# Row numbers of the gathered experts from one sum over two key numbers, the first kept scaled by 128, in a two-layer decoder kernel on one core

## Chip, core and metric

The kernel runs on one core of one Trainium2 chip. The metric is device time of one execution in microseconds (us), lower is better. The engines are named as in the profile: PE (TensorE, matrix products; PEld its weight loads), DVE (VectorE), ACT (ScalarE), POOL (GpSimd) and SP, which only starts transfers.

## What is computed

Two layers: RWKV time mixing, then a pooling mixer, each followed by an expert layer ("PEER") with 8 heads. The change is in the expert layers alone. A head scores two sets of 128 keys, keeps the best 16 of each, adds them pairwise and keeps the best 16 of the 256 sums. Each kept pair names one of 16384 experts, and the expert's number is first key times 128 plus second key:

```
s_top, i_top = lax.top_k(s, K)
cand = (s_top[..., 0, :, None] + s_top[..., 1, None, :]).reshape(B, S, PEER_HEADS, K * K)
cand_idx = (i_top[..., 0, :, None] * N_KEYS + i_top[..., 1, None, :]).reshape(B, S, PEER_HEADS, K * K)
best, pos = lax.top_k(cand, K)
idx = jnp.take_along_axis(cand_idx, pos, axis=-1)
gate = jax.nn.softmax(best, axis=-1).astype(h.dtype)
...
u_sel = jnp.take(u_tab, ix, axis=0)
act = jax.nn.gelu(jnp.einsum('thkd,td->thk', u_sel, hx), approximate=False)
v_sel = jnp.take(v_tab, ix, axis=0)
return jnp.einsum('thk,thkd->td', gx * act, v_sel)
```

## The kernel before

`phase_peer` runs once per layer (tiles named `peer0...`, `peer1...`). Tokens lie on 128 partitions in four tiles. For the first two and a half token tiles nothing is gathered: all 128 tiles of the table U are multiplied with the tokens on PE (`u_product`, L2076, 24 products of 320 columns for each tile e), and the gates are spread into a dense matrix later. For the last tile (GT) and half of the one before (OT) the rows of U are gathered: POOL starts an indirect transfer for each of the head's numbers (`fetch_u`, L2297, 512 KB into one of 8 buffers `row`) and DVE multiplies each row with its token (`dot`, L2381).

In the first 56 tiles the eight heads run beside this, one for each HEAD_TILES = 7 tiles. For head n:

- PE makes the query (L2053 to L2055), one u_product, then the scores (L2062), then six more u_products. ACT takes the scores into `sc` (L2180); windows below are cut at these moments.
- For each tile ACT rounds U into `uhi` (L2168) and POOL makes the remainder `ulo` (L2320, in `low_u`), which u_product waits for. POOL's order is fixed: a remainder, then one to three `fetch_u`; twice in a head also the remainder of the next query's weights `wlo` (L2326, right behind an `ulo`).
- DVE looks for the best 16 of both sides (L2412 to L2416), adds the pairs (L2428), turns the key numbers `pos` into bfloat16 `posf` (L2431), looks for the best 16 pairs, and finds each pair's two ranks (L2436 to L2445). Then for s = 0, 1: a 0/1 mask of ranks (L2448), times the key numbers or their steps `posd` (L2450), summed over 16 (L2451) into `slots[:, 1 + s]`. L2452 makes first number x 128 + second, L2454 adds the layer's offset and stores integers in `idx`, which signals `idx_made`. Twelve dots of a previous head are laid between these steps by `fill`.

DVE's order is written out: the next head starts with a search (L2412) and then one dot. `fetch_u(m)` waits for the head's numbers and for the dot eight before it, since there are NG = 8 buffers. So POOL, in front of a fetch, can wait for a dot of DVE, and PE waits behind POOL for the remainder.

After the heads `slots` is turned by PE, and ACT takes it into `slotT` (`take_slots`, L2194), where `slotT[:, 1]` must be the plain first key number: DVE compares it with 0 to 127 (L2480).

Of the kernel before, what the change touches and what calls it, by code (L numbers as in the profile page):

```python
# [15 lines left out]
ALU = mybir.AluOpType  # L16
ACT = mybir.ActivationFunctionType
AX = mybir.AxisListType

P = 128  # L20
HEAD = 64
TOPK = 16
# [1736 lines left out]
def phase_peer(nc, made, const, arena, kept, pe_t, name, layer, w_q, keysT, uT, u_rows, v_tab, v_rows, mod_rows, w_dram, gelu_dram,  # L1759
# [4 lines left out]
    with ExitStack() as ctx:  # L1764
# [4 lines left out]
        DT, GT = TT - 1, TT - 1  # L1769
        SD = DT * P  # L1770
        HEADS = w_q.shape[0]
        SLOTS = HEADS * TOPK
        ET = uT.shape[0]
# [69 lines left out]
        slotT = arena("slotT", [P, 3, SD])  # L1843
# [33 lines left out]
        posf, posd = early("posf", [P, 2, TT, TOPK + 2], BF16), early("posd", [P, TT, TOPK], BF16)  # L1877
        starts = early("starts", [P, 2, TOPK])
        best, bpos = early("best", [P, TT, TOPK]), early("bpos", [P, TT, TOPK], U32)
        half_u, half_f = early("half_u", [P, 2, TT * TOPK], U32), early("half_f", [P, 2, TT * TOPK])  # L1880
        total = early("total", [P, TT * HEADS])
        slots = early("slots", [P, 3, TT, SLOTS])
        idx_f = early("idx_f", [P, 2, TOPK])
        h_rows = [kept["gate"], kept["g_row"]]
# [54 lines left out]
        with nc.Block() as block:  # L1939
# [216 lines left out]
            def _(act):  # L2156
# [35 lines left out]
                def take_slots(q):  # L2192
                    act.wait_ge(slots_turned, q + 1)
                    a.activation(slotT[:, q], four[q % 2][:, 0:SD], ACT.Copy).then_inc(slotT_made, 1)  # L2194

# [165 lines left out]
            def _(dve):  # L2361
# [7 lines left out]
                ch.send(v.tensor_tensor(h_own, x_own, h_rows[0][:], ALU.add))  # L2369
                ch.send(v.memset(posf[:, :, :, 0:2], 0.0))  # L2370
                ch.send(v.tensor_scalar(starts[:, 1], const["iota"][:, 0:TOPK], float(FULL_ROWS * (FULL_ROWS - 1)), None, ALU.add))
                ch.wait()
# [45 lines left out]
                for n in range(HEADS):  # L2418
# [7 lines left out]
                    for rows_of, cols_of, to in ((slice(0, FULL_ROWS), TOPK, slice(0, at)), (slice(FULL_ROWS, TOPK), FULL_ROWS, slice(at, CAND))):  # L2426
# [3 lines left out]
                                                val[:, 1, :, 0:cols_of].unsqueeze(2).to_broadcast(shape), ALU.add))  # L2430
                    v.tensor_copy(posf[:, :, :, 2:], pos[:]).then_inc(less_made, 1)  # L2431
                    ch.wait()
# [13 lines left out]
                    for s, (ranks, op, by) in enumerate(((starts[:, 0], ALU.is_le, posd[:]), (const["iota"][:, 0:TOPK], ALU.is_equal, posf[:, 1, :, 2:]))):  # L2446
# [4 lines left out]
                        ch(v.tensor_reduce(slots[:, 1 + s, :, col], hot[:, s], AX.X, ALU.add))  # L2451
                    ch(v.scalar_tensor_tensor(out=idx_f[:], in0=slots[:, 1, OT:GT + 1, col], scalar=float(P), in1=slots[:, 2, OT:GT + 1, col],  # L2452
                                              op0=ALU.mult, op1=ALU.add))
                    v.tensor_scalar(idx[:, :, col], idx_f[:], float(layer * ET * P), None, ALU.add).then_inc(idx_made, 1)  # L2454
                v.sem_inc(all_less, 1)
# [216 lines left out]
```

## Time and profile before

| | us |
|---|---|
| median of 3 runs | 3241.31 (3236.23 to 3244.79) |
| the profiled execution | 3236.63 |
| its span, first to last instruction | 3234.8 |
| PE busy | 3041.8 |
| DVE busy | 2671.3 |
| POOL busy | 2173.7 |
| ACT busy | 1413.9 |
| heads and what follows up to the softmax, layer 0 | 601 to 942 |
| the same, layer 1 | 1987 to 2328 |

A row of the profile gives a busy time; for DVE and POOL that includes time in which a started instruction doesn't get on. So the same instruction's shortest and longest durations are worth comparing. A wait that hangs on several signals is put down to the one that came last by the profile, which need not be the one that mattered.

### The profile page before, as it was taken

What the parts mean: (1) busy time and instruction counts of PE and PEld (TensorE: products, weight loads), DVE (VectorE), ACT (ScalarE), POOL (GpSimd) and SP (SyncE); (2) the same over time, 40 slices, a digit from 0 to 9 for tenths busy, and PEclk for the clock granted to TensorE, in tenths of its full rate; (3) what the DMA queues carried; (4) which work ended last, traced back from release to release, by engine and by line L of the source; (5) the groups of instructions that cost most, each with busy time, mean ns of one, the idle gap of its engine ahead of it and who ended that gap; (6) DMA issues with size and microseconds to landing.
All of it is one profiled execution on the core that took longest, in us unless ns stands there. A gap on an engine that the chain in (4) does not pass through costs nothing. (4 is left out here: it accounts for less than half of the span.)

```text
span 3234.8 us, 58229 instructions
## 1 busy us (share of the span) xinstructions
PE 3041.8 (94%) x21401; PEld 2588.8 (80%) x21401; DVE 2671.3 (83%) x4637; ACT 1413.9 (44%) x2848; POOL 2173.7 (67%) x1430
## 2 busy tenths in 40 slices
PE   8999998999988889999999899999898899999998
PEld 3347887788888889888888677888888898888886
DVE  8775663699998775999999656899988768999997
ACT  0124553433347776333333423333377763333333
POOL 1223543588887777888888505888877678888884
PEclk9999999999999999999999999999999999999999
DMA  9950011588888999999999505888889999999994
GB/s 343 323 192 16 4 52 51 194 315 294 276 297 320 368 372 339 362 339 338 356 337 338 202 29 163 305 298 279 285 309 368 387 336 362 337 337 353 339 337 172
DMA packets 370430, 891.65 MB, mean 276 GB/s; under 512 B 39769, under 2 KB 191889, under 8 KB 363026
## 3 DMA queue, kind: packets, MB, share of 16 engines
q1 hardware_dynamic: 266514, 511.04, 45.4%
q0 software_dynamic: 103680, 377.53, 32.2%
q8 instruction: 139, 2.28, 0.3%
q14 instruction: 97, 0.79, 0.1%
HBM read 801.19 MB, written 86.03 MB: 274 GB/s over the span
## 5 line engine op out<-in xcount | busy, mean ns | idle before, releaser
L2076 PE MATMUL peer_acc<-peer_hhi,peer_uhi 128*128 128x320 f32 x2048 | 657.1, 321 | 42.0 <-POOL peer0same_ulo L2320 22.1
L2076 PE MATMUL peer_acc<-peer_hlo,peer_uhi 128*128 128x320 f32 x2048 | 642.4, 314 | 0.0
L2381 DVE SCALAR_TENSOR_TENSOR peer_row<-peer_row,peer_acc 128x1024 f32<-128x1024 f32 x384 | 462.8, 1209 | 91.1 <-DMA peer_row<-in_pe_u,peer_idx 84.7
L2076 PEld LDWEIGHTS peer_acc<-peer_hhi,peer_uhi 128*128 128x128 f32 x2048 | 394.4, 193 | 51.1 <-POOL peer0same_ulo L2320 26.1
L2076 PEld LDWEIGHTS peer_acc<-peer_hlo,peer_uhi 128*128 128x128 f32 x2048 | 394.1, 192 | 1.0 <-issue 0.5
L2320 POOL TENSOR_TENSOR peer1same_ulo<-ahead_u,peer_uhi 128x1024 fp32r<-128x1024 f32 x128 | 314.8, 2462 | 100.9 <-ACT peer_uhi L2168 97.3
L2320 POOL TENSOR_TENSOR peer0same_ulo<-ahead_u,peer_uhi 128x1024 fp32r<-128x1024 f32 x128 | 313.8, 2455 | 99.1 <-ACT peer_uhi L2168 93.4
L2349 POOL TENSOR_TENSOR peer1lsame_vlo<-peer1l_v,peer_uhi 128x1024 fp32r<-128x1024 f32 x128 | 308.6, 2411 | 76.3 <-ACT peer_uhi L2217 75.7
L2349 POOL TENSOR_TENSOR peer0lsame_vlo<-peer0l_v,peer_uhi 128x1024 fp32r<-128x1024 f32 x128 | 308.4, 2409 | 75.2 <-ACT peer_uhi L2217 74.1
L2392 DVE SCALAR_TENSOR_TENSOR peer_acc<-peer_row,peer_p_g,peer_acc 128x1024 f32<-128x1024 f32 x254 | 324.5, 1278 | 18.4 <-DMA peer_row<-in_pe_v,peer_idx 18.0
L2076 PE MATMUL peer_acc<-peer_hhi,peer1same_ulo 128*128 128x320 f32 x1024 | 321.5, 314 | 0.0
L2076 PE MATMUL peer_acc<-peer_hhi,peer0same_ulo 128*128 128x320 f32 x1024 | 320.0, 312 | 0.0
L2119 PE MATMUL peer_acc<-peer_uhi,peer1p_phi 128*128 128x512 f32 x768 | 299.4, 390 | 4.3 <-DVE peer1lo_plo L2508 2.8
L2119 PE MATMUL peer_acc<-peer_uhi,peer0p_phi 128*128 128x512 f32 x768 | 299.2, 390 | 3.7 <-DVE peer0lo_plo L2508 2.3
L2119 PE MATMUL peer_acc<-peer_uhi,peer1lo_plo 128*128 128x512 f32 x768 | 298.8, 389 | 0.0
L2119 PE MATMUL peer_acc<-peer1lsame_vlo,peer1p_phi 128*128 128x512 f32 x768 | 298.8, 389 | 0.0
L2119 PE MATMUL peer_acc<-peer0lsame_vlo,peer0p_phi 128*128 128x512 f32 x768 | 298.8, 389 | 0.0
L2119 PE MATMUL peer_acc<-peer_uhi,peer0lo_plo 128*128 128x512 f32 x768 | 298.8, 389 | 0.0
L2297 POOL DMA_INDIRECT peer_row<-in_pe_u,peer_idx x256 | 257.1, 1004 | 59.7 <-issue 51.2
L2297 POOL DMA_INDIRECT peer_row<-in_pe_v,peer_idx x256 | 261.2, 1020 | 38.9 <-issue 9.3
L2164 ACT ACTIVATE peer_gel<-peer_acc 128x320 f32<-128x320 f32 x256 | 110.1, 430 | 398.8 <-PE peer_acc L2076 385.5
L2168 ACT ACTIVATE peer_uhi<-ahead_u 128x1024 fp32r<-128x1024 f32 x250 | 262.1, 1048 | 0.0
(522 smaller groups left out, 7241.5 us busy)
## 6 DMA issues: line engine op xcount, KB each, us to landing
ahead_u<-in_pe_uT SPq DMA_DIRECT2D x256, 512.0 KB
peer0l_v<-in_pe_v SPq DMA_DIRECT2D x128, 512.0 KB
peer1l_v<-in_pe_v SPq DMA_DIRECT2D x128, 512.0 KB
activations<-peer_gel SPq DMA_DIRECT2D x256, 160.0 KB
rw_g<-in_ada POOLq DMA_DIRECT2D x60, 512.0 KB
routing<-peer0m_wb SPq DMA_DIRECT2D x20, 1024.0 KB
peer0l_wt<-routing SPq DMA_DIRECT2D x64, 320.0 KB
routing<-peer1m_wb SPq DMA_DIRECT2D x20, 1024.0 KB
```

The lines of the kernel that those rows point to most:

```text
L2076: mm = pe.matmul(ub[e % 2][:, 0:UD], a, h[:, k, 0:UD], start=(n == 0), stop=(n == 3 * KT - 1))
L2119: mm = pe.matmul(acc[:, t, ds], a[:, ts], w[:, ds], start=(begin and n == 0), stop=(end and n == 2), skip_group_check=True)
L2164: a.activation(gel[:, e % NL], ub[e % 2][:, 0:UD], ACT.Gelu).then_inc(gel_made, 1)
L2168: a.activation(uhi[:, n % NH], u[:, n % NU], ACT.Copy).then_inc(uhi_made, 1)
L2297: g.indirect_dma_start(row[:, at % NG], None, table, bass.IndirectOffsetOnAxis(ap=of, axis=0)).then_inc(row_loaded[at % NG], 16)
L2320: g.tensor_tensor(ulo[:, q].rearrange("p k e -> p (k e)"), u[:, q].rearrange("p k e -> p (k e)"), uhi[:, e % NH].bitcast(F32).rearrange("p ...
L2349: g.tensor_tensor(vlo[:, q], vr[:, q], vhi[e % NH].bitcast(F32), ALU.subtract).then_inc(vlo_made, 1)
L2381: v.scalar_tensor_tensor(out=row[:, m % NG], in0=row[:, m % NG], scalar=1.0, in1=h_own if mine else h_g, op0=ALU.mult, op1=ALU.mult, accum ...
L2392: v.scalar_tensor_tensor(out=acc_g, in0=row[:, at % NG], scalar=p_g[:, s:s + 1], in1=acc_g, op0=ALU.mult, op1=ALU.add).then_inc(acc_made, 1)
```

## The change

The first key number is scaled when it becomes a float: `posf[:, 0]` is now key x 128 plus layer x 16384, in an instruction of its own (`tensor_scalar`), and `posf[:, 1]` in another (`tensor_copy`); before, one instruction made both. All these values are whole numbers of at most 8 significant bits times a power of two, so bfloat16 holds them. The steps `posd`, the mask products and the sums work as before on the scaled numbers. The expert's number is then one `tensor_reduce` over the two sums, stored as integers, in place of two instructions with a wait between. `slotT[:, 1]` is scaled back by ACT, with Identity, a scale of 1/128 and a bias from `first_key`, a [128, 1] tile set once in each layer.

```diff
-        starts = early("starts", [P, 2, TOPK])
+        starts, first_key = early("starts", [P, 2, TOPK]), early("first_key", [P, 1])
...
                     act.wait_ge(slots_turned, q + 1)
-                    a.activation(slotT[:, q], four[q % 2][:, 0:SD], ACT.Copy).then_inc(slotT_made, 1)
+                    if q == 1:
+                        a.activation(slotT[:, q], four[q % 2][:, 0:SD], ACT.Identity, scale=1.0 / P, bias=first_key[:]).then_inc(slotT_made, 1)
+                    else:
+                        a.activation(slotT[:, q], four[q % 2][:, 0:SD], ACT.Copy).then_inc(slotT_made, 1)
...
                 ch.send(v.memset(posf[:, :, :, 0:2], 0.0))
+                ch.send(v.memset(first_key[:], float(-layer * ET)))
...
-                    v.tensor_copy(posf[:, :, :, 2:], pos[:]).then_inc(less_made, 1)
+                    v.tensor_copy(posf[:, 1, :, 2:], pos[:, 1])
+                    v.tensor_scalar(posf[:, 0, :, 2:], pos[:, 0], float(P), float(layer * ET * P), ALU.mult, ALU.add).then_inc(less_made, 1)
...
-                    ch(v.scalar_tensor_tensor(out=idx_f[:], in0=slots[:, 1, OT:GT + 1, col], scalar=float(P), in1=slots[:, 2, OT:GT + 1, col],
-                                              op0=ALU.mult, op1=ALU.add))
-                    v.tensor_scalar(idx[:, :, col], idx_f[:], float(layer * ET * P), None, ALU.add).then_inc(idx_made, 1)
+                    with nc.allow_low_precision(reason="whole numbers below 2 ** 24, exact in float32, kept as integers"):
+                        v.tensor_reduce(idx[:, :, col], slots[:, 1:3, OT:GT + 1, col].rearrange("p s t k -> p t k s"), AX.X,
+                                        ALU.add).then_inc(idx_made, 1)
```

DVE, layer 1, end of a head and start of the next, before (`hot` is the mask, `slots` the sums, `peer_row` a gathered row):

```order
L2450 TENSOR_TENSOR peer1a_hot<-peer1a_hot,peer1a_posf 128x1024
L2451 TENSOR_REDUCE peer1a_slots<-peer1a_hot 128x4x16
L2452 SCALAR_TENSOR_TENSOR peer1a_idx_f<-peer1a_slots 128x32
L2454 TENSOR_SCALAR peer_idx<-peer1a_idx_f 128x2x16
L2412 MAX peer1a_val<-peer1a_sc 128x8 x4
L2381 SCALAR_TENSOR_TENSOR peer_row,peer_dots<-peer_row,peer_acc 128x1024
```

The same place after (line numbers are 3 to 4 higher):

```order
L2454 TENSOR_TENSOR peer1a_hot<-peer1a_hot,peer1a_posf 128x1024
L2455 TENSOR_REDUCE peer1a_slots<-peer1a_hot 128x4x16
L2457 TENSOR_REDUCE peer_idx<-peer1a_slots 128x2x16
L2415 MAX peer1a_val<-peer1a_sc 128x8 x4
L2384 SCALAR_TENSOR_TENSOR peer_row,peer_dots<-peer_row,peer_acc 128x1024
```

Two instructions of DVE have become one, of another kind; the search and the first dot follow it as before.

DVE in the middle of a head of layer 1, after, where one CAST of 128x8x16 (L2431) stood between the pair sums and the search:

```order
L2431 TENSOR_TENSOR kept_b_row<-peer1a_val 128x4x64
L2431 TENSOR_TENSOR kept_b_row<-peer1a_val 128x4x48
L2434 CAST peer1a_posf<-peer1a_pos 128x4x16
L2435 TENSOR_SCALAR peer1a_posf<-peer1a_pos 128x4x16
L2415 MAX peer1a_best<-kept_b_row 128x8 x4
```

One instruction more. ACT, layer 0, behind the heads (`peer0a_slots` is the softmax's exponential), after:

```order
L2264 ACTIVATE peer0a_slots<-peer0a_slots 128x512
L2163 ACT_TABLE_LOAD
L2163 ACTIVATE peer_gel<-peer_acc 128x320
L2167 ACTIVATE peer_uhi<-ahead_u 128x1024
L2196 ACTIVATE peer_slotT<-peer_acc 128x384
L2194 ACTIVATE peer_slotT<-peer_acc,peer0a_first_key 128x384
```

The table load stood there before too; none is added. The orders of PE, POOL and SP are unchanged, and `first_key`'s memset in each layer is the only other new instruction.

## Rows read from the trace of the kernel before

**Rows 1.** The page, the chain that ended last, by line.
```profile
PE peer_acc L2119 15%; DVE peer_row L2381 3%; PE peer_acc L2076 3%; POOL peer_row L2297 2%; DMA peer_row<-in_pe_u,peer_idx 1%; POOL peer1same_ulo L2320 1%; DVE peer1a_idx_f L2452 1%; DVE peer1a_hot L2448 1%; PE peer_acc L2051 0%; DVE peer1a_slots L2451 0%; DVE peer1a_pos L2416 0%; DVE peer1a_pos L2414 0%; DVE kept_g_row L2413 0%; DMA kept_g_row<-activations 0%; DVE kept_b_row L2428 0%
```

**Rows 2.** Busy time of each engine in windows from scores taken to scores taken.
```profile
core 0: us, PE busy (x) PEld busy (x) DVE busy (x) ACT busy (x) POOL busy (x), PEclk, DMA share, GB/s
681.50:719.68 38.18, 37.59 (x235) 35.43 (x234) 37.87 (x136) 13.79 (x22) 33.82 (x21) 1.00 0.91 310
719.68:886.99 167.31, 155.53 (x931) 146.19 (x930) 165.70 (x551) 55.12 (x82) 136.75 (x84) 0.97 0.85 288
2066.58:2104.74 38.16, 37.58 (x235) 35.42 (x234) 37.82 (x137) 13.79 (x22) 33.39 (x21) 1.00 0.92 311
2104.74:2272.94 168.20, 158.03 (x931) 149.12 (x930) 166.58 (x552) 55.13 (x82) 136.50 (x84) 0.95 0.85 286
2272.94:2328.24 55.30, 49.26 (x328) 47.66 (x327) 53.75 (x145) 19.09 (x29) 47.57 (x27) 1.00 0.86 304
```

**Rows 3.** Timeline of DVE (start, us, ...) from one head's start to the next's.
```profile
2115.59 0.87 DVE L2412 MAX8 peer1a_val<-peer1a_sc 128x8 f32<-128x128 f32 x4
...
2148.41 2.06 DVE L2448 TENSOR_TENSOR peer1a_hot<-const_made,peer1a_half_f 128x1024 bf16<-128x1024 f32 x1
...
2152.48 4.91 DVE L2452 SCALAR_TENSOR_TENSOR peer1a_idx_f<-peer1a_slots 128x32 f32<-128x32 f32 x1
...
2157.52 0.86 DVE L2412 MAX8 peer1a_val<-peer1a_sc 128x8 f32<-128x128 f32 x4
2158.30 1.20 DVE L2381 SCALAR_TENSOR_TENSOR peer_row<-peer_row,peer_acc 128x1024 f32<-128x1024 f32 x1
```

**Rows 4.** Timeline of POOL over the same place, and one of the tail.
```profile
2152.56 2.42 POOL L2320 TENSOR_TENSOR peer1same_ulo<-ahead_u,peer_uhi 128x1024 fp32r<-128x1024 f32 x1
2154.94 2.40 POOL L2326 TENSOR_TENSOR peer1aover_wlo<-ahead_wq,peer1aover_whi 128x1024 fp32r<-128x1024 f32 x1
2160.29 0.95 POOL L2297 DMA_INDIRECT peer_row<-in_pe_u,peer_idx_own  x1 [2.95 <-DMA peer_idx_own<-peer_idx]
...
2284.47 0.95 POOL L2297 DMA_INDIRECT peer_row<-in_pe_u,peer_idx_own  x1 [2.96 <-DVE peer_row L2381]
```

**Rows 5.** Timeline of PE: the gap behind POOL in two heads.
```profile
2085.22 0.41 PE L2076 MATMUL peer_acc<-peer_hhi,peer_uhi 128*128 128x320 f32 x1 [0.58 <-POOL peer1same_ulo L2320]
...
2163.67 0.41 PE L2076 MATMUL peer_acc<-peer_hhi,peer_uhi 128*128 128x320 f32 x1 [2.71 <-POOL peer1same_ulo L2320]
```

**Rows 6.** DVE's groups by line: xcount | busy us, mean ns | idle before.
```profile
L2452 DVE SCALAR_TENSOR_TENSOR peer0a_idx_f<-peer0a_slots 128x32 f32<-128x32 f32 x8 | 25.0, 3127 | 0.3
L2452 DVE SCALAR_TENSOR_TENSOR peer1a_idx_f<-peer1a_slots 128x32 f32<-128x32 f32 x8 | 23.6, 2945 | 0.3
```

**Rows 7.** Line L2451: duration ns min/median/max, first and last start, forms.
```profile
L2451 DVE TENSOR_REDUCE peer1a_slots<-peer1a_hot x16: 1219/1220/1222, 2014.8 to 2322.7; 128x64 f32<-128x1024 bf16 x16
```

**Rows 8.** Timelines of DVE and POOL in the head in front, layer 1.
```profile
2071.16 0.19 DVE L2452 SCALAR_TENSOR_TENSOR peer1a_idx_f<-peer1a_slots 128x32 f32<-128x32 f32 x1
...
2089.96 2.90 DVE L2428 TENSOR_TENSOR kept_b_row<-peer1a_val 128x256 f32<-128x256 f32 x2
...
2101.83 0.22 DVE L2436 TENSOR_TENSOR peer1a_slots<-peer1a_best 128x64 f32<-128x64 f32 x1
...
2089.89 2.40 POOL L2320 TENSOR_TENSOR peer1same_ulo<-ahead_u,peer_uhi 128x1024 fp32r<-128x1024 f32 x1
```

**Rows 9.** Timeline of DVE: other instructions held up, first and last head.
```profile
2002.08 2.44 DVE L2431 CAST peer1a_posf<-peer1a_pos 128x128 bf16<-128x128 uint32 x1
...
2319.86 2.78 DVE L2450 TENSOR_TENSOR peer1a_hot<-peer1a_hot,peer1a_posf 128x1024 bf16<-128x1024 bf16 x1
```

**Rows 10.** Timelines of DVE and ACT behind the last head.
```profile
2330.20 0.69 DVE L2460 TENSOR_REDUCE peer1a_total<-peer1a_slots 128x32 f32<-128x512 f32 x1 [2.87 <-ACT peer1a_slots L2262]
...
2328.24 1.28 ACT L2262 ACT_TABLE_LOAD   x1
```

More of the change, by code:

```diff
@@ L1882, in phase_peer @@
         slots = early("slots", [P, 3, TT, SLOTS])
-        idx_f = early("idx_f", [P, 2, TOPK])
         h_rows = [kept["gate"], kept["g_row"]]
```

## Prediction

> **What bounds the kernel now.** I read the page's chain first. A line that only turns 512 sums into 256 numbers, L2452, holds 1% of the span in it, as much as a line with far more work [rows 1]. Its group says why: 16 instructions take 25.0 + 23.6 = 48.6 us, 3.0 us each for 32 numbers [rows 6], while the undisturbed one takes 0.19 us [rows 8]. So about 48.6 - 16 x 0.19 = 45.6 us of DVE's time are spent standing, spread over both layers.
>
> The timelines say what it stands for. In the head that begins at 2115.59, L2452 starts at 2152.48 and lasts 4.91 us, to 2157.39 [rows 3]. POOL runs two subtractions without a break from 2152.56 to 2157.34 [rows 4]. DVE goes on when POOL's second one ends. L2451, the sum over one tensor just ahead of it, takes 1.219 to 1.222 us in all of its cases, in every head and whatever POOL does [rows 7]; L2452, L2450, L2448 and L2431 are the ones with long cases [rows 3, 9]. What is held up is an instruction that reads two tensors, or a copy; a sum over one tensor isn't.
>
> Next, who waits for DVE. The windows from scores to scores tell it: four heads take 168.20 us in layer 1, with DVE busy 166.58 of them, PE 158.03, POOL 136.50 [rows 2]. DVE is the engine without idle time. The way to PE leads through POOL: the next head's first dot (L2381) starts at 2158.30 and ends 1.2 us later, and POOL starts the fetch that needs its buffer at 2160.29, 2.95 us late. The profile puts that down to the move of the numbers, but the same wait in another head is put down to the dot (2.96), and 2158.30 + 1.20 + 0.79 = 2160.29 [rows 3, 4]; I take the dot. POOL's remainder then comes late and PE stands 2.71 us [rows 5]. In these four heads PE's granted clock is 0.95 on average, some of the time at its 1.2 GHz level, against 1.00, all at 2.4 GHz, in the head in front [rows 2]. I don't count that apart, since it lies inside the windows' difference.
>
> **A head without the stall** is in the trace: in the head whose L2452 took 0.19 us [rows 8] the next scores came after 38.16 us, in layer 0 after 38.18 [rows 2]; PE's gap was 0.58 us [rows 5]. The following four take 168.20 / 4 = 42.05 and 167.31 / 4 = 41.83 us. These two quiet windows are my yardstick.
>
> **Part by part.**
> Removed, L2452: 0.19 us of own time and the standing in it, 4.72 us in the head of rows 3.
> Removed, L2454: own time 0.18, of which 2157.52 - 2157.39 = 0.13 us lies on the path [rows 3].
> Added, the sum into `idx`: 64 elements read. The nearest rows are a sum over 512 numbers, 0.69 us [rows 10], and one over 1024, 1.22 us [rows 7]; a line through both gives 0.16 us fixed and 1.04 ns a number, so 0.22 us. Its bounds are 0.1 us and 0.69 us, the upper one because its two inputs lie far apart in memory, which no row shows. I take 0.22: even 0.69 would cost 8 x 0.5 us a layer of slack that isn't used up (below). By rows 7 it doesn't stand behind POOL; if it does, that is the second rival.
> Added, a second instruction for `posf`: 0.1 us between two starts, as L2454 to the next. Below nothing it can't be, since work is added; above, an instruction of this place (L2431) has taken 2.44 us [rows 9], 2.2 more than when free. I take 0.13 and keep 2.2 for a rival.
> Added on ACT: Identity with a scale and a bias for one copy of PSUM per layer. No table load is added in the order; if one were, it would be 1.28 us [rows 10], so 0 to 2.6 us in all. I take 0. The memset per layer is far ahead of any wait: 0.
>
> DVE's own time per head, from search to search: 2157.52 - 2115.59 = 41.93 [rows 3]. Of it 4.72 is L2452's stall, and L2448 took 2.06 where the free mask takes 1.22, so 0.84. That leaves 36.37, and the edits make 36.37 - 0.19 - 0.13 + 0.22 + 0.13 = 36.4 us. So DVE alone could do a head in 36.4, and PE and POOL do one in 38.2. DVE can stand 1.8 us per head elsewhere before it sets the time again.
>
> Will it stand more? I follow the phases. Count from the moment at which scores are taken. The quiet head ends for DVE at about 2110.6 + 0.3, 6.1 us behind the scores of 2104.74 (the stall of 4.7 us then made it 10.85: 2115.59). L2428 stood at 18.5 us after its head's start, 2089.96, against a subtraction of POOL that ran 23.3 to 25.7 us behind the scores (2089.89, 2.40 long) [rows 8]. With a lag of 6.1 DVE comes there at 24.6 and stands 1.1 us. The closing row of small instructions (L2436) starts 9.65 us of work later, at 6.1 + 28.15 + 1.1 - 38.2 = 2.85 us ahead of the next scores; in the quiet head that was 2104.74 - 2101.83 = 2.91, and what followed there was the 0.84 us at L2448, in the head of rows 3 too. Sum 1.9 us, so the next lag is 6.1 + 36.4 + 1.9 - 38.2 = 6.2. A larger lag misses POOL's subtraction at L2428 and shrinks; a smaller one meets more of it and grows. The phase holds itself, and DVE is then just not the bound. POOL's first fetch that needs a dot comes 2157.5 - 2146.4 = 11.1 us behind the scores, and the dot is done and seen 2.8 us after the head's start, so any lag below 8.3 us leaves POOL free.
>
> **What is late next** is PE with POOL: 38.2 us, plus 0.2 that I allow for DVE's longer `posf` and for phases that are not just those of the quiet head. The sum:
> layer 0, four heads: 167.31 - 4 x 38.4 = 13.7 us;
> layer 1, four heads: 168.20 - 4 x 38.4 = 14.6 us;
> the stretch of 55.30 us behind the last scores in each layer [rows 2]: POOL's wait of 2.96 in it goes [rows 4], and POOL sets the pace of the tiles there, so up to 3.0 us; I take 2 in each, 4 us.
> Together 32 us. The first three heads keep their times. What stands behind the heads starts earlier and has no other change. Against its own execution that is 3236.6 - 32.3 = 3204.3 us. That execution lies 4.7 us below the median of the runs (3241.3), so for a median I say **3209 us**.
>
> **The rivals.**
> First, the phase doesn't hold and half of the gain is eaten: L2428, L2448 and L2450 stand 3 to 4 us a head in place of 1.9, DVE needs 36.4 + 3.5 = 39.9. For it: in the heads at both ends of each layer such stalls are common (2.22 at L2428 in rows 8; 2.09 at L2450 and 2.2 at L2431 in rows 9). The eight heads take 167.31 + 168.20 = 335.5 now, so 335.5 - 8 x 39.9 = 16 us: 3225.
> Second, no change: the stall moves. POOL's double subtraction is still there, and the instruction ahead of L2452, the product L2450, can meet it, or the new sum stands as L2452 did. At 5.5 us a head DVE needs 41.9 as now, and 3241 stays. For it: 0.84 + 4.72 = 5.56 is just what it stands now, so a mere move gives nothing. Against it: the sum over one tensor never stood [rows 7], and from a lag of 6 the product is done some 2 us before the double subtraction begins.
> A rule of the Trainium skill leads to the same end by another way. "VectorE: DVE Perf Modes", section "Rules for kernel authors", says that chained operations of this engine are not to be fused for speed, and that the number of operations is what to cut; it adds that a reduce is the slowest kind. Per head the change takes away three (a copy, L2452, L2454) and puts in three. By that count it would be worth nothing. The rows speak against the count as a measure here: what goes is not an operation's own 0.2 us.
> Third, slower. The extra instruction for `posf` and a lag that grows meet: if a head in front loses so much that DVE starts over 8.3 us behind the scores, POOL is held again, and if L2450 comes to stand for both subtractions, there are still 1.22 + 0.22 us of sums behind it, where now only L2452's last 0.2 us follow. The head would need about 42 + 1.2, ten heads 12 us more, plus 2.2 us where `posf` is caught: 3255. The point is a lag of 8.3 in place of 6.1, so 2.2 us more of stalls in one head than the quiet one had (2.22 at L2428 and 0.84 at L2448). Beside this stands a rule of the skill, "SBUF — State Buffer", section "SBUF: two separate sides": VectorE and GpSimd share a port pair that one of them holds for a whole instruction, and copies that use both read ports need it as well. That is why a second copy is a second chance to be caught; it gives no price that the rows lack.
> Fourth, more than the forecast: PE's gap and POOL's holds go entirely, heads take PE's own 37.6 [rows 2]: 335.5 - 300.8 = 34.7 and 6 in the tails, 41 us: 3200.
>
> **How the numbers follow.** My forecast (3204 to 3219; the ends are 38.0 us a head with 6 us in the tails, and 39.2 with none) has 0.5, the first rival 0.18, no change 0.15, slower 0.09, more than the forecast 0.08. A change within 0.3%, 10 us, is about what a measurement of this kernel can't tell from none. Faster by more: 0.5 + 0.08 + 0.18 = 0.76; within: 0.15; slower: 0.09. The range leaves out the slower case and the half of no change that lies above: 3199 to 3238.
>
> **What would show it.** The new sum (L2457) in 0.2 us in all 16 heads. Windows between scores of 38 to 38.6 us from the fourth head on, PE's clock back at 1.00 where its gap falls from 2.7 to about 0.6. POOL's 2.95 us in front of a fetch gone. DVE with gaps or with under 2 us of stalls per head at L2431, L2452 and L2454 of the new file. I am wrong if L2457 has cases of 2 us and more (second rival), if the products and masks show the 4.7 us instead (second or third), or if the heads shorten and the tiles behind them lengthen.

## The result: slower by 27 us, and the profile after

The kernel before takes 3239.46 us (median of 4 runs, 3236.23 to 3244.79), the changed one 3266.7 us (median of 4, 3264.8 to 3272.68). The ratio is 1.0085, with a 95% interval of 1.0072 to 1.0098: slower by 0.85%, some 27 us, where the prediction said 3209 and gave "slower" a chance of 0.09. The profiled execution of the changed kernel took 3264.8 us with a span of 3263.0 us.

The lines of the change come first. The two sources L2452 and L2454 of before are gone. In their place stands L2457, and the one copy for `posf` is now L2434 (copy, second keys) and L2435 (scaled, first keys). From the views of single lines (durations in ns as min/median/max, then the first and last start):

```profile
L2457 DVE TENSOR_REDUCE peer_idx<-peer0a_slots x8: 222/224/229, 633.7 to 951.8; 128x32 uint32<-128x64 f32 x8
L2457 DVE TENSOR_REDUCE peer_idx<-peer1a_slots x8: 222/224/228, 2038.1 to 2353.3; 128x32 uint32<-128x64 f32 x8
...
L2435 DVE TENSOR_SCALAR peer0a_posf<-peer0a_pos x8: 180/3020/3032, 620.5 to 929.0; 128x64 bf16<-128x64 uint32 x8
L2435 DVE TENSOR_SCALAR peer1a_posf<-peer1a_pos x8: 181/3022/3032, 2022.9 to 2331.1; 128x64 bf16<-128x64 uint32 x8
```

The sum is as cheap as was estimated, 0.22 us in all 16 heads. The scaled half of `posf` has 64 elements per partition and takes 0.18 us when nothing is in its way, but its median is 3.02 us. That is a stall of 2.84 us, in the same five of the eight heads of each layer (the third to the seventh), with next to no spread between them.

The windows from scores to scores say where the time goes. The columns are as in [rows 2]: window, us, busy time of each engine, PE's granted clock, DMA share, GB/s.

```profile
680.42:718.58 38.16, 37.59 (x235) 35.43 (x234) 38.06 (x129) 13.79 (x21) 33.34 (x21) 1.00 0.90 313
718.58:897.30 178.72, 158.04 (x931) 149.40 (x930) 177.21 (x553) 55.13 (x81) 137.25 (x84) 0.92 0.80 269
897.30:957.90 60.60, 53.10 (x328) 51.77 (x327) 53.96 (x154) 19.10 (x29) 46.24 (x27) 0.92 0.81 278
2082.78:2120.92 38.14, 37.58 (x235) 35.42 (x234) 38.04 (x129) 13.79 (x21) 33.37 (x21) 1.00 0.91 312
2120.92:2299.72 178.80, 158.91 (x931) 150.27 (x930) 177.29 (x555) 55.14 (x81) 137.21 (x84) 0.92 0.81 270
2299.72:2357.60 57.88, 50.63 (x328) 49.02 (x327) 53.05 (x152) 19.09 (x29) 46.95 (x27) 0.97 0.84 289
```

Against [rows 2], the head in front of the four is unchanged (38.16 and 38.14 against 38.18 and 38.16). The four heads take 178.72 and 178.80 where they took 167.31 and 168.20, so 11.4 and 10.6 us more. The stretch behind the last scores takes 60.60 and 57.88 instead of 55.30, so 5.3 and 2.6 more. Together that is 29.9 us; the spans differ by 3263.0 - 3234.8 = 28.2. A head now lasts 178.8 / 4 = 44.7 us, with DVE busy 177.3 of 178.8, so DVE is still the engine without idle time. PE's clock is 0.92 on average in these heads (0.97 and 0.95 before), more of the time at its 1.2 GHz level, after longer gaps.

What stands in one of these heads is in DVE's timeline (start, us, engine, line). First the place where `posf` is made, then the closing block:

```profile
2197.93 0.70 DVE L2431 TENSOR_TENSOR kept_b_row<-peer1a_val 128x256 f32<-128x256 f32 x2
...
2198.54 0.20 DVE L2434 CAST peer1a_posf<-peer1a_pos 128x64 bf16<-128x64 uint32 x1
2198.64 3.03 DVE L2435 TENSOR_SCALAR peer1a_posf<-peer1a_pos 128x64 bf16<-128x64 uint32 x1
...
2211.18 2.28 DVE L2447 TENSOR_SCALAR peer1a_half_u<-peer1a_half_u 128x64 uint32<-128x64 uint32 x1
...
2217.25 2.53 DVE L2452 TENSOR_TENSOR peer1a_hot<-const_made,peer1a_half_f 128x1024 bf16<-128x1024 f32 x1
2219.82 2.78 DVE L2454 TENSOR_TENSOR peer1a_hot<-peer1a_hot,peer1a_posf 128x1024 bf16<-128x1024 bf16 x1
2222.62 1.22 DVE L2455 TENSOR_REDUCE peer1a_slots<-peer1a_hot 128x64 f32<-128x1024 bf16 x1
2223.88 0.22 DVE L2457 TENSOR_REDUCE peer_idx<-peer1a_slots 128x32 uint32<-128x64 f32 x1
```

and POOL beside it:

```profile
2197.99 1.20 POOL L2299 DMA_INDIRECT peer_row<-in_pe_u,peer_idx_own  x1 [0.16 <-issue]
2199.21 2.40 POOL L2322 TENSOR_TENSOR peer1same_ulo<-ahead_u,peer_uhi 128x1024 fp32r<-128x1024 f32 x1
...
2216.30 2.41 POOL L2322 TENSOR_TENSOR peer1same_ulo<-ahead_u,peer_uhi 128x1024 fp32r<-128x1024 f32 x1 [0.24 <-ACT peer_uhi L2167]
2218.66 3.38 POOL L2328 TENSOR_TENSOR peer1aover_wlo<-ahead_wq,peer1aover_whi 128x1024 fp32r<-128x1024 f32 x1
2226.78 0.95 POOL L2299 DMA_INDIRECT peer_row<-in_pe_u,peer_idx_own  x1 [4.74 <-DMA peer_idx_own<-peer_idx]
```

L2435 starts at 2198.64, inside the fetch that began at 2197.99, and ends at 2201.67, with the subtraction that ended at 2201.61. So it stood through the rest of the fetch and the whole subtraction. In the closing block of the same head three instructions stand, with their free durations beside them: L2447 2.28 (0.19 for its like), L2452 2.53 (1.22), L2454 2.78 (0.69). The stalls are 2.1, 1.3 and 2.1, so 5.5 us in place of the 5.56 of before (4.72 at old L2452 and 0.84 at L2448, [rows 3]). The standing at the key numbers has gone, and nearly the same amount has come back in front of the sums. The extra 2.84 comes on top. With 36.4 us of own work that makes 36.4 + 2.8 + 5.5 = 44.7, the mean of the four measured heads (this one takes 44.56 from search to search, 2179.46 to 2224.02). POOL now waits 4.74 us at the fetch that needs the first dot (2.95 before, [rows 4]), and PE's gap behind it is 4.82 us (2.71 before, [rows 5]):

```profile
2230.17 0.63 PE L2075 MATMUL peer_acc<-peer_hhi,peer_uhi 128*128 128x320 f32 x1 [4.82 <-POOL peer1same_ulo L2322]
```

### The profile page after: what moved, and what is told of

Same layout as the page of the kernel before. It is cut to its first block and busy times, and to the rows that moved or that the text cites. A ratio compares the mean times of both kernels' runs of the same rounds, so it can differ in the third digit from the quotient of the medians.

```text
span 3263.0 us, 58231 instructions
## 1 busy us (share of the span) xinstructions
PE 3046.2 (93%) x21401; PEld 2593.0 (79%) x21401; DVE 2700.4 (83%) x4639; ACT 1413.6 (43%) x2848; POOL 2168.5 (66%) x1430
## 3 DMA queue, kind: packets, MB, share of 16 engines
q8 instruction: 139, 2.28, 0.3%
## 5 line engine op out<-in xcount | busy, mean ns | idle before, releaser
L2075 PE MATMUL peer_acc<-peer_hhi,peer_uhi 128*128 128x320 f32 x2048 | 660.3, 322 | 63.1 <-POOL peer0same_ulo L2322 32.1
L2075 PE MATMUL peer_acc<-peer_hlo,peer_uhi 128*128 128x320 f32 x2048 | 645.5, 315 | 0.0
L2075 PEld LDWEIGHTS peer_acc<-peer_hhi,peer_uhi 128*128 128x128 f32 x2048 | 397.6, 194 | 70.8 <-POOL peer0same_ulo L2322 35.4
L2075 PEld LDWEIGHTS peer_acc<-peer_hlo,peer_uhi 128*128 128x128 f32 x2048 | 397.5, 194 | 1.0 <-issue 0.5
L2075 PE MATMUL peer_acc<-peer_hhi,peer0same_ulo 128*128 128x320 f32 x1024 | 322.5, 315 | 0.0
L2075 PE MATMUL peer_acc<-peer_hhi,peer1same_ulo 128*128 128x320 f32 x1024 | 322.1, 315 | 0.0
L2299 POOL DMA_INDIRECT peer_row<-in_pe_u,peer_idx x256 | 250.2, 978 | 59.6 <-issue 51.0
```

Of the source, the lines that this page charges most:

```text
L2075: mm = pe.matmul(ub[e % 2][:, 0:UD], a, h[:, k, 0:UD], start=(n == 0), stop=(n == 3 * KT - 1))
L2299: g.indirect_dma_start(row[:, at % NG], None, table, bass.IndirectOffsetOnAxis(ap=of, axis=0)).then_inc(row_loaded[at % NG], 16)
```

## The experiments

My theory after the result had two parts. The one sum is worth what was predicted. The second `posf` instruction costs more than that, because it stands for POOL's fetch and the subtraction behind it. The rivals were that the sum is the cause, that the number of instructions is, or that any extra instruction in this place has this price. Eight kernels were run. The kernel before ran beside them and gave medians of 3241.22, 3242.56 and 3238.41 us. All kernels compute the whole result.

| kernel | key numbers | `posf` | us | ratio to before (95%) |
|---|---|---|---|---|
| changed kernel | one sum | copy, then scaled | 3266.7 | 1.0085 (1.0072 to 1.0098) |
| split_only | as before | copy, then times 1 | 3271.19 | 1.0097 (1.0081 to 1.0114) |
| one_posf | one sum | one product | 3210.28 | 0.9906 (0.9889 to 0.9922) |
| late_scale | one sum | one copy, differences scaled later | 3216.19 | 0.9924 (0.9907 to 0.9941) |
| swap_posf | one sum | scaled, then copy | 3266.12 | a single run |
| posf_first | one sum | copy and scaled, ahead of the pair sums | 3209.1 | 0.989 (0.9873 to 0.9906) |
| split_reduce | as before | copy, then a sum over an axis of one | 3244.76 | 1.0006 (0.9996 to 1.0015) |
| one_first | one sum | one product, ahead of the pair sums | 3209.5 | 0.9897 (0.9881 to 0.9914) |
| late_split | one sum | copy, then a sum over an axis of one | 3211.66 | 0.9917 (0.99 to 0.9933) |

### split_only: the split without the sum

From the kernel before:

```diff
-                    v.tensor_copy(posf[:, :, :, 2:], pos[:]).then_inc(less_made, 1)
+                    v.tensor_copy(posf[:, 1, :, 2:], pos[:, 1])
+                    v.tensor_scalar(posf[:, 0, :, 2:], pos[:, 0], 1.0, 0.0, ALU.mult, ALU.add).then_inc(less_made, 1)
```

> The kernel before with one edit: posf is made by two instructions (a copy and a tensor_scalar times 1), the numbers still by L2452 and L2454. Theory A (the second instruction is what costs: POOL's fetch and the subtraction behind it get in between the two): the tensor_scalar lasts about 3.0 us in the middle heads, heads of 43.5 us or more, some 10 x 2 to 10 x 2.9 us slower than before, 3258 to 3268. Theory B (the loss comes from taking L2452 away, whose wait kept DVE and POOL in a good phase): within 5 us of 3239.

It measured 3271.19 us, so 30 us slower than before with this one edit, and 3 us over the range expected. The split alone carries the whole loss, and it costs slightly more than the changed kernel. DVE's groups (busy us, mean ns | idle before) show something unexpected too:

```profile
L2432 DVE TENSOR_SCALAR peer1a_posf<-peer1a_pos 128x64 bf16<-128x64 uint32 x8 | 17.9, 2239 | 0.0
...
L2453 DVE SCALAR_TENSOR_TENSOR peer1a_idx_f<-peer1a_slots 128x32 f32<-128x32 f32 x8 | 2.4, 298 | 0.3
```

L2453 is the instruction that held 4.7 us per head before (mean 2945 ns, [rows 6]). Here it is still in the program, and it takes 298 ns. Its long wait left it without being taken out: after its stand at `posf`, DVE comes to the closing block 2.8 us later than before in relation to POOL, so POOL's subtractions met the mask and the product ahead of it (L2449 at 2.71, L2451 at 2.78 us in the head of 2174.82) and a small instruction (L2445, 2.41 us). This is why the changed kernel gets nothing from removing it: where a second instruction stands at `posf`, L2452 has no wait left to remove.

### one_posf: the sum without the split

From the changed kernel, with a tile `key_by` of two columns that holds 128 and 1, and the layer's offset in a column of `posf` that is read for the first difference:

```diff
+                ch.send(v.memset(posf[:, 0, :, 1:2], float(-layer * ET * P)))
...
-                    v.tensor_copy(posf[:, 1, :, 2:], pos[:, 1])
-                    v.tensor_scalar(posf[:, 0, :, 2:], pos[:, 0], float(P), float(layer * ET * P), ALU.mult, ALU.add).then_inc(less_made, 1)
+                    v.tensor_tensor(posf[:, :, :, 2:], pos[:], key_by[:].unsqueeze(2).unsqueeze(3).to_broadcast([P, 2, TT, TOPK]),
+                                    ALU.mult).then_inc(less_made, 1)
```

> The changed kernel with one edit: posf is made by one instruction again, a tensor_tensor of pos with a [128, 2] tile that holds 128 and 1; the layer's offset comes in through the zero column in front of the steps. The numbers still come from one sum. Theory A: heads of 38.2 to 38.6 us from the fourth on, 3205 to 3215 in all, as I had predicted for the whole change. Theory B: the wait moves into the closing block (5.4 us a head there, as in the changed kernel), heads of 41.5 us or more, 3235 to 3267.

It measured 3210.28 us, 31 us faster than before, with the same result as the changed kernel. This is close to the 3209 that the prediction gave to the change. All four heads and one of them:

```profile
2129.10:2167.99 38.89, 37.85 (x235) 35.43 (x234) 38.51 (x138) 13.79 (x22) 34.25 (x21) 1.00 0.91 316
2090.17:2245.74 155.57, 151.41 (x931) 141.71 (x930) 154.06 (x549) 55.16 (x82) 136.90 (x84) 1.00 0.89 310
```

A head takes 38.9 us with PE at full clock; the prediction had 38.4, and 38.6 was the most expected before the run. The two layers' four heads take 155.57 and 155.00 us, the stretches behind them 52.92 and 52.93. Against [rows 2] that is 12.6 + 12.3 + 2.4 + 2.4 = 29.7 us less; the spans differ by 28.4.

With split_only this fills a table of four, each against the kernel before that ran beside it: the sum without the split -31; the split alone +30; both +27. If the effects added, both together would give -1. They don't add: what the sum saves is saved only while DVE's lag behind the scores stays small, and a second instruction that stands makes it large.

### late_scale: one copy, the scale put elsewhere

From the changed kernel:

```diff
+                ch.wait()
+                ch.send(v.memset(posf[:, 0, :, 1:2], float(-layer * ET)))
...
-                    v.tensor_copy(posf[:, 1, :, 2:], pos[:, 1])
-                    v.tensor_scalar(posf[:, 0, :, 2:], pos[:, 0], float(P), float(layer * ET * P), ALU.mult, ALU.add).then_inc(less_made, 1)
+                    v.tensor_copy(posf[:, :, :, 2:], pos[:]).then_inc(less_made, 1)
...
                     ch(v.tensor_tensor(posd[:], posf[:, 0, :, 2:], posf[:, 0, :, 1:TOPK + 1], ALU.subtract))
+                    ch.send(v.tensor_scalar(posd[:], posd[:], float(P), None, ALU.mult))
```

> The changed kernel with the scaling at another place: one copy makes posf unscaled, as before the change, and a tensor_scalar of 64 numbers multiplies the steps posd by 128 in the closing block, where several short instructions follow each other. As many instructions as in the changed kernel. Theory A: the place counts, not the number; no 3 us at posf, heads near 38.5 to 39, 3205 to 3220. Theory B: 3235 to 3267. A third theory, that one more instruction anywhere costs: about as the changed kernel, 3260 to 3270.

It measured 3216.19 us, with heads of 38.9 us. This kernel has as many DVE instructions per head as the changed one, and the scaling is an instruction of its own as there. At its new place it stands in one head of eight in each layer (2.28 us; the mean is 444 ns, the median 182). So neither the number of instructions nor the scaling costs the 27 us; the place does.

### swap_posf: the same two, the other way round

```diff
+                    v.tensor_scalar(posf[:, 0, :, 2:], pos[:, 0], float(P), float(layer * ET * P), ALU.mult, ALU.add)
+                    v.tensor_copy(posf[:, 1, :, 2:], pos[:, 1]).then_inc(less_made, 1)
```

> The changed kernel with the two instructions for posf in the other order, the tensor_scalar first. Theory A says the second one, now the copy, lasts 3.0 us in the middle heads and the time stays 3265. If it is the kind of instruction that is held up, the tensor_scalar has the long cases in first place too, and the copy none.

It measured 3266.12 us in a single run, as the changed kernel. The long cases changed their owner:

```profile
L2435 DVE CAST peer0a_posf<-peer0a_pos 128x64 bf16<-128x64 uint32 x8 | 17.9, 2242 | 0.0
...
L2434 DVE TENSOR_SCALAR peer0a_posf<-peer0a_pos 128x64 bf16<-128x64 uint32 x8 | 3.8, 470 | 0.0
```

In the third to the seventh head of each layer, whichever of the two comes second lasts 3.02 us and the first 0.2. As between a copy and a scaling, it is the second place and not the kind.

### posf_first: the same two, some 0.7 us earlier

The two `posf` lines of the changed kernel are moved ahead of the pair sums, and nothing else.

> The changed kernel with its two instructions for posf put ahead of the two pair sums (L2431) instead of behind them; nothing else. Theory A1 (it is the order of asking: POOL's fetch starts with DVE's row of four instructions, needs the port about half a microsecond later, and gets it at the first gap between two instructions that it has asked before): at that time DVE is in its last long pair sum, after which DVE asks for nothing, so there is no 2.85 us at posf; heads of 38.5 to 39, 3208 to 3220. Theory A2 (a fourth instruction in the row is one too many, wherever it stands): the last of the four stands 2.8 us and the time stays 3260 to 3270.

It measured 3209.1 us, 58 us below the changed kernel, with the same instructions (the profiled execution was the slowest of its four, 3219.74 us). From the second head of each layer on, the copy now stands for the subtraction that is already running (in place of the pair sums behind it), and the scaled one takes 0.18 us. DVE and POOL in one head (layer 1; start, us):

```profile
2161.66 2.41 POOL L2322 TENSOR_TENSOR peer1same_ulo<-ahead_u,peer_uhi 128x1024 fp32r<-128x1024 f32 x1
2162.38 1.75 DVE L2428 CAST peer1a_posf<-peer1a_pos 128x64 bf16<-128x64 uint32 x1
2164.05 0.18 DVE L2429 TENSOR_SCALAR peer1a_posf<-peer1a_pos 128x64 bf16<-128x64 uint32 x1
2164.15 0.68 DVE L2433 TENSOR_TENSOR kept_b_row<-peer1a_val 128x256 f32<-128x256 f32 x2
2164.23 1.16 POOL L2299 DMA_INDIRECT peer_row<-in_pe_u,peer_idx_own  x1 [0.16 <-issue]
```

When the fetch starts, both `posf` instructions are done. Behind the pair sums comes a search, which POOL doesn't hold up (the searches over `kept_b_row`, one by one, take 250 to 268 ns in all 64 cases of the changed kernel). This is the cleanest run against the rival that counts instructions. A rule of the Trainium skill leads to that rival: "VectorE: DVE Perf Modes", section "Rules for kernel authors", says to minimise the count of operations. By that rule the changed kernel and posf_first would take the same time; they differ by 58 us at the same count.

### split_reduce: the split, with a second instruction of another kind

From the kernel before:

```diff
-                    v.tensor_copy(posf[:, :, :, 2:], pos[:]).then_inc(less_made, 1)
+                    v.tensor_copy(posf[:, 1, :, 2:], pos[:, 1])
...
+                        v.tensor_reduce(posf[:, 0, :, 2:], pos[:, 0].unsqueeze(3), AX.X, ALU.add).then_inc(less_made, 1)
```

> The kernel before with posf made by two instructions as in split_only, but the second one is a tensor_reduce over an axis of one element, a kind that has never stood behind POOL. L2452 and L2454 are there. If the port is what the second instruction waits for: it takes 0.2 us in every head, POOL is not disturbed, and the time is that of the kernel before within 5 us, 3237 to 3247, with L2452 standing 4.7 us again. If the number of instructions or the phase alone does it: 3260 to 3275 as split_only.

It measured 3244.76 us, no change from before, where the same split with a scaling cost 30 us. The sum that makes `posf` takes 209 ns on average in layer 1, and nearly the same in layer 0. The groups of the closing block:

```profile
L2454 DVE SCALAR_TENSOR_TENSOR peer1a_idx_f<-peer1a_slots 128x32 f32<-128x32 f32 x8 | 9.6, 1202 | 0.3
...
L2452 DVE TENSOR_TENSOR peer1a_hot<-peer1a_hot,peer1a_posf 128x1024 bf16<-128x1024 bf16 x8 | 18.1, 2261 | 0.3
```

The main point is confirmed, in the slow heads as well. There the copy and the second instruction start 0.53 and 0.63 us into a fetch (0.55 and 0.65 in the changed kernel, at 2197.99), and nothing stands:

```profile
2183.67 1.17 POOL L2297 DMA_INDIRECT peer_row<-in_pe_u,peer_idx_own  x1 [0.16 <-DVE peer_row L2381]
2184.20 0.19 DVE L2431 CAST peer1a_posf<-peer1a_pos 128x64 bf16<-128x64 uint32 x1
2184.30 0.21 DVE L2433 TENSOR_REDUCE peer1a_posf<-peer1a_pos 128x64 bf16<-128x64 uint32 x1
```

The part of my expectation about the closing block isn't confirmed. I had expected L2454 (L2452 of before) to stand 4.7 us a head again, but it lasts 1.2 on average, and the two products now take the rest (2.84 and 2.79 us in the head of 2154.20, free 0.69). The stalls of these three are 2.15 + 2.10 + 0.84 = 5.1 us (a small instruction, L2445, adds 0.2), and the head takes 41.74 us, about what it took before. The sum over an axis of one costs about 0.1 us to the next start, so a shift that small is enough to hand the standing to other instructions of the block. That is argued, and no run shows it. I didn't predict it, and I don't know how to do so closer than "about 5 us somewhere".

### one_first: control for the move

one_posf with its instruction ahead of the pair sums.

> The kernel one_posf (one sum for the numbers, posf by one instruction) with that instruction ahead of the pair sums. It asks whether order alone still has something to give when no instruction stands at posf: heads in one_posf take 38.9 us, of which PE's own work is 37.3. I expect 3205 to 3213, the same as one_posf within 3 us, since DVE's waits are covered there; a phase that meets POOL at another place could cost up to 20 us.

It measured 3209.5 us, the same as one_posf. The move by itself is worth nothing; in posf_first it was worth 58 us, because there it took a standing instruction from its place.

### late_split: both, with the kind that doesn't stand

split_reduce left a doubt. Its closing block stood at other instructions than before, so a split of any kind might destroy the sum's gain. late_split is late_scale with its one copy made of two instructions.

```diff
-                    v.tensor_copy(posf[:, :, :, 2:], pos[:]).then_inc(less_made, 1)
+                    v.tensor_copy(posf[:, 1, :, 2:], pos[:, 1])
...
+                        v.tensor_reduce(posf[:, 0, :, 2:], pos[:, 0].unsqueeze(3), AX.X, ALU.add).then_inc(less_made, 1)
```

> This is late_scale with its one CAST for the key numbers made of two instructions: a copy for the second half and, for the first, a sum over an axis of one. The arithmetic is the same. So it holds what the changed kernel holds (a second instruction of that place, the one sum), and both instructions per head more than late_scale's one; only the second instruction is of the kind that was never seen to stand. Theory A (the loss of the changed kernel comes from the second instruction standing for POOL's fetch and the subtraction behind it, the sum's gain is there whenever nothing stands in that place): the sum over an axis of one takes 0.21 us in every head, the heads stay at 38.8 to 39.2 us, and the time is 3212 to 3224, within 0.3% of late_scale's 3216. Theory B (with two instructions there the one sum gives nothing, because DVE's lag is then another and the stall comes back in the products of the closing block, as it did in split_reduce): heads of 41 to 42 us, 3236 to 3250. If the time lies at 3226 to 3235, both hold in part of the heads.

It measured 3211.66 us (3212 to 3224 was expected), with heads of 38.9 us (2093.01, 2131.89, 2170.83 are the scores). So the split doesn't harm; a second instruction that stands does. This trace can be laid beside the changed kernel's where DVE and POOL stand alike to each other. First the changed kernel, in the last head ahead of its slow ones (scores at 2082.78), DVE and POOL:

```profile
2105.99 3.06 DVE L2431 TENSOR_TENSOR kept_b_row<-peer1a_val 128x256 f32<-128x256 f32 x2
2106.09 2.40 POOL L2322 TENSOR_TENSOR peer1same_ulo<-ahead_u,peer_uhi 128x1024 fp32r<-128x1024 f32 x1
2108.65 0.96 POOL L2299 DMA_INDIRECT peer_row<-in_pe_u,peer_idx_own  x1 [0.16 <-issue]
2108.97 0.18 DVE L2434 CAST peer1a_posf<-peer1a_pos 128x64 bf16<-128x64 uint32 x1
2109.07 3.02 DVE L2435 TENSOR_SCALAR peer1a_posf<-peer1a_pos 128x64 bf16<-128x64 uint32 x1
2109.62 2.40 POOL L2322 TENSOR_TENSOR peer1same_ulo<-ahead_u,peer_uhi 128x1024 fp32r<-128x1024 f32 x1
```

Then late_split:

```profile
2155.98 2.41 POOL L2322 TENSOR_TENSOR peer1same_ulo<-ahead_u,peer_uhi 128x1024 fp32r<-128x1024 f32 x1
2156.68 2.27 DVE L2433 TENSOR_TENSOR kept_b_row<-peer1a_val 128x256 f32<-128x256 f32 x2
2158.55 0.96 POOL L2299 DMA_INDIRECT peer_row<-in_pe_u,peer_idx_own  x1 [0.16 <-issue]
2158.88 0.18 DVE L2436 CAST peer1a_posf<-peer1a_pos 128x64 bf16<-128x64 uint32 x1
2158.98 0.21 DVE L2438 TENSOR_REDUCE peer1a_posf<-peer1a_pos 128x64 bf16<-128x64 uint32 x1
2159.53 2.42 POOL L2322 TENSOR_TENSOR peer1same_ulo<-ahead_u,peer_uhi 128x1024 fp32r<-128x1024 f32 x1
```

In both, the pair sums wait for a subtraction and end 0.4 us after POOL has begun its next fetch (in this profile a row of DVE can begin 0.1 us before the one ahead of it ends). So the copy starts 0.32 and 0.33 us into the fetch, and the second instruction 0.42 and 0.43. The scaling then lasts 3.02 us, to the end of the next subtraction; the sum lasts 0.21. The rest of the place is the same, but for the time that the pair sums waited (3.06 and 2.27 us long) and the scaling, which late_split has in the closing block. This pair of traces, with the pair of slow heads under split_reduce, shows the mechanism.

The heads in which L2435 doesn't stand say more about what it waits for. This is the changed kernel's second head of layer 1:

```profile
2065.72 0.96 POOL L2299 DMA_INDIRECT peer_row<-in_pe_u,peer_idx_own  x1 [0.16 <-issue]
2066.14 0.18 DVE L2435 TENSOR_SCALAR peer1a_posf<-peer1a_pos 128x64 bf16<-128x64 uint32 x1
2066.98 0.94 POOL L2299 DMA_INDIRECT peer_row<-in_pe_u,peer_idx_own  x1 [0.30 <-issue]
```

It starts 0.42 us into a fetch, just as at 2109.07, and takes 0.18 us; the same in the last head of both layers (929.01 in a fetch from 928.59, 2331.12 in one from 2330.70). What differs is POOL's order: a second fetch comes next there, and in the third to the seventh head the subtraction does. So a running fetch alone doesn't hold the instruction up. It stands where a subtraction is next behind the fetch.

## Why the prediction was wrong, step by step

**The bound, and what stands for what: right.** DVE was the engine without idle time, L2452 stood for POOL's double subtraction, and the way to PE led through the first dot. All this is borne out by one_posf, which takes out L2452 and L2454 as the change does, keeps one instruction for `posf`, and gains 31 us.

**The new sum: right.** Estimated at 0.22 us and never standing; measured 0.222 to 0.229 in all 16 heads. **The copy of PSUM on ACT and the memsets: right**, in so far as one_posf, which has them too, comes out at 3210.

**The second `posf` instruction: the step that failed.** The prediction took 0.13 us for it and kept "2.2 for a rival". It measured 2.84 us above its free 0.18 in ten heads of 16, and 2.27 in one more. Two things were wrong. The first is the size: 2.2 us came from a copy that stood for a subtraction [rows 9], but here the instruction stands for what is left of a fetch and then for the whole of the subtraction behind it. The second, which matters more, is the likelihood. I took the stall as an accident of the phase, and I had worked out that phase myself: DVE stands at L2428 until POOL's subtraction ends. What follows is fixed then. In [rows 8] L2428 starts at 2089.96 and lasts 2.90, to 2092.86, behind a subtraction that ends at 2092.29. POOL starts its next fetch 0.17 us after that end, at 2092.46, and DVE the copy 0.32 us after that, at 2092.78. The slow heads of the kernel before have the same meeting, though DVE doesn't stand at L2428 there. These lines were in the trace, and the prediction didn't read them:

```profile
2134.15 1.17 POOL L2297 DMA_INDIRECT peer_row<-in_pe_u,peer_idx_own  x1 [0.16 <-DVE peer_row L2381]
2134.68 0.21 DVE L2431 CAST peer1a_posf<-peer1a_pos 128x128 bf16<-128x128 uint32 x1
```

An instruction put there doesn't meet the fetch by chance, but in each of the third to the seventh head; in the second and the last of both layers L2435 took its free 0.18, since POOL has another fetch next and not the subtraction. The copy of before was at this very place and escaped, because nothing that POOL can hold up came behind it: next was a search.

**The phases: right only without that stall.** The prediction said that the lag (from the scores to DVE's first search) holds itself at about 6 us, with some 1.9 us of stalls a head. In one_posf the lag is 6.3 us in layer 1's four heads (2096.47 - 2090.17 in the first). The stalls are 2.6 us and not 1.9, 1.55 at the pair sums (below, 0.70 when free), 0.84 at the mask and 0.2 at a small instruction, which is why its heads take 38.9 us and not 38.4. In the changed kernel the lag goes from 4.7 to 13.8 us in a single head, the one that has its scores at 2082.78: the pair sums stand 2.4 us, L2435 2.8, a small instruction 2.2, and the mask 3.5, for both of POOL's subtractions:

```profile
2153.86 2.25 DVE L2436 TENSOR_TENSOR kept_b_row<-peer1a_val 128x256 f32<-128x256 f32 x2
...
2127.91 4.69 DVE L2452 TENSOR_TENSOR peer1a_hot<-const_made,peer1a_half_f 128x1024 bf16<-128x1024 f32 x1
```

(The first line is one_posf's, the second the changed kernel's.) That is beyond the 8.3 us that the prediction had named as the point from which POOL is held. From there the lag stays at 13.2 us (13.9 once, in layer 0) and the block stands some 5.5 us. That was the third rival's mechanism, with the right point, but at 0.09 and priced at 3255 instead of 3267; it had let the product stand for both subtractions, and it was the mask, in one head of layer 1 and two of layer 0. It had priced the stalls at the level of before plus 1.2 us of sums, and 2.2 once "where `posf` is caught". The head took 44.7 us and not 42 + 1.2, since `posf` is caught in every one of these. The eight heads inside the windows make 22.0 us of it (11.4 + 10.6), the stretches behind them 7.9.

**No change through a moved stall**, the second rival, was half of what happened: the stall did move, into a small instruction, the mask and the product (5.5 us in place of 5.56). Together with `posf`'s 2.84 that explains both the lost gain and the loss.

**The clock.** The prediction left it inside the windows' difference, and the result bears that out: 1.00 in the heads of 38.9 us, 0.95 to 0.97 in those of 42 and 0.92 in those of 44.7. PE's idle time behind POOL at L2075 is 63.1 us over the run, against 42.0 before and 24.6 in one_posf:

```profile
L2075 PE MATMUL peer_acc<-peer_hhi,peer_uhi 128*128 128x320 f32 x2048 | 660.3, 322 | 63.1 <-POOL peer0same_ulo L2322 32.1 <-POOL peer1same_ulo L2322 30.8
```

**What stays open.** Every stall here is read from durations; no record shows who holds the port. The fetch lasts 0.96 us at 2108.65 and 1.20 at 2197.99, where it began earlier against DVE's row of short instructions. In both heads L2435 starts 0.54 to 0.55 us ahead of the fetch's end and stands, and the copy, 0.1 us earlier, doesn't. That the instruction is kept out on behalf of the subtraction, before this has begun, is inferred from the heads with two fetches, where nothing stands; no run changed POOL's order or moved the fetch alone. Why a subtraction passes an instruction of DVE that already waits, as the second one passed old L2452 (4.72 us), is not explained either; in the closing block at 2217.25 the two engines took turns instead, and POOL's second subtraction (L2328, 3.38 us for a free 2.40) waited for the mask. That a phase repeats from head to head, because the first dot releases POOL and both engines then run fixed sequences, is argued from the timelines; no run delayed one engine alone.

## What to carry to other kernels

Before an instruction is split or added beside another engine that shares its port, look at what the other engine starts at that moment and next. If your instruction stands behind its operation there, or the two engines start together in each round, the next one of that engine can be due at a fixed distance, and what you put second then meets it round after round (here in five heads of eight, for 0.18 us of work). Put the short instructions ahead of the one that waits, follow the last one by a kind that isn't held up, or use a kind that isn't (here the sum over an axis of one). And a change whose gain rests on a small lag has to be counted together with all that the edit adds: here -31 and +30 us made +27.

## What the runs showed of the hardware

- The same 64 elements per partition take 0.18 or 3.02 us as a scaling in the second place, just as long as a copy there (swap_posf), and 0.21 us as a sum over an axis of one, at the same moment behind the fetch's start (2109.07 and 2158.98 above). The Trainium skill, "SBUF — State Buffer", section "SBUF: two separate sides", says that VectorE in its fast modes or with two inputs in SBUF and GpSimd take a shared port pair as an exclusive lock, held for the whole instruction. The traces agree as to which kinds are held; the sums, with one input, took 222 to 229 ns in 16 of 16 cases. They don't show the lock for the whole of a fetch: the copy gets through in 0.18 us when it starts 0.32 us behind the fetch's start (2108.97), and the scaling at 2066.14 does, 0.42 us behind it, where another fetch follows.
- A fetch by indirect DMA, 0.95 us long on POOL, is itself held up by DVE. It lasts 1.15 to 1.20 us where DVE's short instructions run in its way (1.20 at 2197.99) and 1.75 us beside a mask (at 2149.54 in the kernel before, where L2448 runs from 2148.41 for 2.06 us), and a subtraction behind it starts without letting a waiting instruction of DVE through.
- A sum can be the cheaper instruction. The page of the Trainium skill that asks for few operations, "VectorE: DVE Perf Modes", section "Rules for kernel authors", calls the reduce the slowest kind. At 64 elements it costs 0.21 us against 0.18, and in late_split and split_reduce, in the place where the scaling or the copy stood, it spared the 2.84 us of standing.
